# A two-layer hybrid decoder trunk on eight cores: a new opening of mixer 2, other load gates, and an order searched by shaking priorities

## The chip, the cores and the metric

The kernel runs on the eight cores of one Trainium2 chip, two dies of four cores. Every core does the same work on one batch element of eight; no core talks to another. The metric is the device time of the slowest core, in microseconds, as the median of several runs. One execution is also profiled, and all durations below are of that one.

## The reference

```python
for i in range(DEPTH):                      # DEPTH = 2
    h = rmsnorm(x, norm_mix_g[i])
    if i % 2 == 0:
        x = x + mlstm_mixer(h, ...)         # matrix memory, chunks with a carried state
    else:
        x = x + gla_mixer(h, ...)           # gated linear attention, chunks with a carried state
    h = rmsnorm(x, norm_ffn_g[i])
    x = x + square(relu(h @ w1[i])) @ w2[i] # D = 1024, D_FF = 4096
return rmsnorm(x, final_norm_g)             # x: (8, 2048, 1024) float32
```

Each mixer projects to q, k (512 wide each), v and an output gate (1024 wide each), runs four heads over the sequence with a state that is carried from chunk to chunk, normalises each head, multiplies by the gate and projects back.

## The kernel before

**Stages.** A core holds its `xT` (1024 x 2048, transposed) in SBUF all the time. Four stages follow one another: mixer 1, FFN of layer 0, mixer 2, FFN of layer 1. The 2048 tokens are cut into 4 groups of 512 and 16 chunks of 128. A mixer (`Mixer.run`) walks the 16 chunks; the state products, the gating and the head norm of a chunk (`S1`, `S2`, `P2a` to `P2c`, `S34`, `Cst`) are a chain across TensorE, VectorE and ScalarE, and projections of later tokens (`v`, `o`, `qk`, `op_`) are put between as filling (`fills`, L1255). Two DMA transposes on SP's queue belong to each chunk: `KX` makes the keys token-major (tiles `ktok_134`, `ktok_135`), `S7` brings the head outputs back (tile `hn` into `xn_44` to `xn_47`, dependency name `hnT`). The gates of the second mixer come from `z_F` (L1072): two matmuls, exponentials on ScalarE and eight scans on VectorE.

**FFN.** An FFN works through steps of 7 matrix products each (a seven-product scheme for 2x2 blocks). The weights come in slabs, one DMA on POOL's queue each, cast from float32 on the way (1 MB read, 512 KB landed), into slots `wraw_76` (slot 0) to `wraw_89` (slot 13); slot 1 is `wraw_77`, slot 4 `wraw_80`, slot 5 `wraw_81`. For each slab VectorE makes three sums (`sums`, tiles `wsum`). The first two steps run inside the last chunk of the mixer (`first_tiles`, L1458). `slot_of` (L1429) names the slot of the n-th slab; `loads` starts a slab as soon as the step that used its slot is over.

**Order.** No engine's order is written out by hand. Every `t.op` and `t.dma` appends a unit with its reads, writes and a cost in ns; `order` (L93) then makes a list schedule: `schedule` (L154) walks simulated time, looks at the next units of each engine in program order (48 on TensorE, ScalarE and VectorE, 24 on POOL, 4 on SP), and takes the ready one with the smallest priority. Priorities start as program order; after each pass `needed` (L139) replaces them by the latest start that the schedule allows. Of 8 passes the one with the earliest simulated end is emitted. Units that start in the first 60 us or the last 36 us keep program order. Each engine then runs its list strictly in that order, with semaphore waits made from the reads and writes alone. Simulated slab loads land at 0.29 KB per ns of a shared rate plus 4 us.

**Around the change.** Before the chunk loop of mixer 2, L1541 issues `z_F(1, 0)`, the q and k of two heads of group 1, then `v(0)`, `o(0)`, `v(1)`; `z_F(1, 1)` and the q and k of head 2 are filling of chunk 0. The out projection's eight loads (`wout_load`, L549, two staging buffers `wst_182` and `wst_183`, each followed by one multiply on VectorE) wait only for a free staging buffer. In `ffn_start` (L1439) slab 0 waits for gate 12 and slab 1 for gate 14; slabs 2 and 3 for the last head output of the mixer, and slabs 4 and 5 for nothing but their slot. Gate i (`Mixer.gate`, L1101) means: the head output of chunk i-1 and the keys of chunk i+1 have landed. The final norm of token groups 0 and 1 (`out_held`, L1563, with `stats_slots`) is hooked to steps 31 to 42 of the last FFN; each pair of rows ends in a store `outT<-xT` on SP's queue.

Of the kernel before, what the change touches and what calls it, by code (L numbers as in the profile page):

```python
# [28 lines left out]
class Trk:  # L29
# [4 lines left out]
    SLACK = 300.0  # L34
    PASSES = 8
    EDGES = 60000.0, 36000.0
    LEAD = dict(pe=-163, act=93, dve=82, pool=0, sp=0)
    HOP = dict(pe=145, act=100, dve=100, pool=120, sp=60)
    WIN = dict(pe=48, act=48, dve=48, pool=24, sp=4)

    def __init__(s, nc, es):
        s.nc, s.es = nc, es
        s.E = {}
        for name, eng in (("pe", nc.tensor), ("act", nc.scalar), ("dve", nc.vector),
                          ("pool", nc.gpsimd), ("sp", nc.sync)):
            s.E[name] = dict(eng=eng, sem=es.enter_context(nc.semaphore("s_" + name)), count=0, waited={})
        s.lastw, s.readers, s.iv, s.ovc = {}, {}, {}, {}
        s.nd = 0
        s.xsem = {}
        s.units, s.open = [], None  # L50

    def reg(s, key, lo, size, n=1, step=0):
        s.iv.setdefault(key, []).extend((lo + i * step, lo + i * step + size) for i in range(n))
# [11 lines left out]
    def op(s, ename, fn, r=(), w=(), ns=200, sig=True):  # L65
        reads = [k for k in r if k[0] != "B"]
        writes = [k for k in r if k[0] == "B"] + list(w)
        if s.open is None:
            s.open = dict(eng=ename, ins=[], r=[], w=[], ns=0, dma=None)
        u = s.open  # L70
        assert u["eng"] == ename
        u["ins"].append((fn, reads, writes, sig))
        u["r"] += reads
        u["w"] += writes
        u["ns"] += ns
        if sig:
            s.units.append(u)
            s.open = None

    def dma(s, qname, pairs, nbytes, r=(), w=(), sem=None):  # L80

        assert s.open is None
        u = dict(eng=qname, ins=[], r=list(r), w=list(w), ns=(950 if qname == "pool" else 450) * len(pairs),
                 dma=(pairs, nbytes), tok=None, xp=None, sem=sem)
        s.units.append(u)
        return u

# [5 lines left out]
    def order(s):  # L93

        lastw, readers = {}, {}
        for n, u in enumerate(s.units):
            preds = set()
            for k in u["r"]:  # L100
                if k in lastw:
                    preds.add(lastw[k])
            for k0 in u["w"]:
                for k in s.ov(k0):
                    if k in lastw:
                        preds.add(lastw[k])
                    preds.update(readers.get(k, ()))
            preds.discard(n)
            u["preds"] = preds
            for k in u["r"]:  # L110
                readers.setdefault(k, []).append(n)
            for k in u["w"]:
                lastw[k] = n
                readers[k] = []
        prio, best = list(range(len(s.units))), None
        for n in range(s.PASSES):
            seq, start, done = s.schedule(prio)
            end = max(done)
            if best is None or end < best[0]:
                best = end, seq  # L120
            prio = s.needed(seq, start, done)
            if not n:
                edges = [(m, -1e9) for m in seq if start[m] < s.EDGES[0]]
                edges += [(m, 1e9) for m in seq if start[m] > end - s.EDGES[1]]
            for m, far in edges:
                prio[m] = m + far
        s.model = best[0]
        return best[1]

    def hop(s, p, e):  # L130

# [145 lines left out]
def build():  # L277
# [22 lines left out]
    t = Trk(nc, es)  # L300
# [47 lines left out]
    wqk, _ = at("wqk", [128, KC, 1024], BF16, W[0])  # L348
# [38 lines left out]
    sd, _ = at("sd", [128, GS], F32)  # L387
# [29 lines left out]
    def slot(layer, g):  # L417
        return (g + 2 * layer) % 4
# [127 lines left out]
            t.dma("pool", [(dst[:, k0:k0 + step, :], v[:, k0:k0 + step, c0:c0 + 1024])],  # L546
                  step * 524288, w=[(nm, hf, k) for hf in range(2) for k in range(k0, k0 + step)])

    def wout_load(layer, k, q):  # L549
        v = (m_wout_d if layer == 0 else g_wout_d).rearrange("(k p) n -> p k n", p=128)  # L550
        i = k % len(wst[layer])
        halves = lambda ap: ap.rearrange("p (a n) -> p a n", n=GS)
        t.dma(q, [(wst[layer][i], halves(v[:, k, :]))], 524288, w=[("wst", layer, i)])
        t.op("dve", lambda e: e.tensor_scalar(
            out=halves(wout[:, k, :]), in0=wst[layer][i], scalar1=ong[:, layer * 8 + k:layer * 8 + k + 1],
            scalar2=None, op0=ALU.mult), r=[("wst", layer, i), ("ong",)], w=[("wout", k)], ns=750)
# [72 lines left out]
    def stats_slots(g, eng="pool"):  # L629
        return [lambda: sq_half(g, 0, eng), lambda: sq_half(g, 1, eng), lambda: sq_sum(g)]  # L630
# [296 lines left out]
    class Mixer:  # L927
# [313 lines left out]
        def qk(s, g, h):  # L1241
            return [lambda: s.qk_F(g, h, 0), lambda: s.qk_F(g, h, 1)]
# [12 lines left out]
        def fills(s, i, extra):  # L1255

            g, c = i // 4, i % 4
            v = s.v(i + 2) if i + 2 < NCH and not (s.m and i < 2) else []
            o = s.o(i + 1) if i + 1 < NCH else []
            ops = s.opq[:{0: 2, 1: 2, 2: 4, 3: 0}[c] if g == NG - 1 else 2]  # L1260
            del s.opq[:len(ops)]
            qk = lambda h: s.qk(g + 1, h)
            if g == 0:
                x = extra.get(i, [])
                if c == 0:
                    return x[:2] + o + x[2:] + v + (qk(2)[1:] if s.m else s.z(1, 1) + qk(2) if s.pre else [])
                if c == 1:
                    if s.m:
                        return o + qk(3)[1:]
                    return x[:2] + o + (qk(3) if s.pre else qk(0) + qk(1) + s.z(1, 1)) + x[2:] + v  # L1270
                if c == 2:
                    return o + v + ([] if s.m or s.pre else qk(2) + qk(3))
                return o + v
            if g < NG - 1 and c == 3:
                return qk(0) + qk(1) + s.z(g + 1, 1) + o + ops + v + qk(2) + qk(3)
            return o + v + ops + extra.get(i, []) if g == 1 and c == 0 else o + ops + v + extra.get(i, [])
# [152 lines left out]
    def slot_of(layer, n):  # L1429


        if layer == 0 and n >= 56:
            return (5, 0, 8, 3, 6, 7, 5, 8)[n - 56]
        i = (0, 4, 1, 5)[n] if n < 4 else (0, 4, 2, 3, 1, 5)[(n - 4) % 6]
        return i if layer == 0 or i == 5 else {0: 9, 4: 10, 1: 11, 2: 12, 3: 13}[i]

    ffn = [Ffn(L, lambda n, L=L: slot_of(L, n), ffn_steps(L)) for L in range(2)]
# [1 line left out]
    def ffn_start(layer):  # L1439

        hooks = {}

        def add(i, ns, fns):
            hooks.setdefault(i, []).extend(zip(ns, fns))
        mx, last, f = mix[layer], [("hnT", slot(layer, 3), 3)], ffn[layer]
        add(12, (-1,), [lambda: f.load(mx.gate(12))])
        add(14, (-1,), [lambda: f.load(mx.gate(14))])
        add(15, (0, 0), [lambda: f.load(last)] * 2)
        st = stats_slots(0)
        add(9, (5, 6), st[:2])  # L1450
        add(11, (0,), st[2:])
        add(11, (1, 2, 3, 4), f.xn_slots(0))
        add(12, (1, 3, 5), stats_slots(1))
        add(13, (1, 2, 3, 4), f.xn_slots(1))
        add(14, (1, 2, 3, 4), f.x_prep(0))
        return hooks

    def first_tiles(layer):  # L1458

        def f():  # L1460
            F = ffn[layer]
            set_ring([0, 1, 2, 3, 6])
            F.hold = True
            F.run(0, 2, {})
            F.hold = False
            for n in range(2):
                F.load()
        return [f]

    def mixer_to_ffn(mx, layer):  # L1470
# [68 lines left out]
    m1.KX(0)  # L1539
    m1.KX(1)  # L1540
    m1.z_F(1, 0)  # L1541
    for fn in m1.qk(1, 0) + m1.qk(1, 1) + m1.v(0) + m1.o(0) + m1.v(1):
        fn()
    set_ring(RING["g"])
    hooks = ffn_start(1)
    for k in range(KC):
        i, n = ((1, 11 + k), (2, k - 2), (3, k - 5))[(k > 1) + (k > 4)]
        hooks.setdefault(i, []).append((n, lambda k=k: wout_load(1, k, "pool")))
    m1.run({NCH - 1: first_tiles(1)}, hooks)
    mixer_to_ffn(m1, 1)  # L1550

# [11 lines left out]
    def out_held(g):  # L1563
        def f(k0):
            for k in range(k0, k0 + 2):
                stt(xT[:, k, tgs(g)], xT[:, k, tgs(g)], gains[:, 32 + k:33 + k], PB[ring["held"][g]][:], ALU.mult,
                    ALU.mult, [("gains",), ("B", ring["held"][g])], [("xT", k, g)], GS)
            store("sp", g, k0, 2, 0, GS)
        return [lambda k=k: f(k) for k in range(0, KC, 2)] + [lambda: free_bank(g)]
# [9 lines left out]

    F1 = ffn[1]  # L1580
    hooks = next_pair(1, 20)
    st, o = stats_slots(0, "dve"), out_held(0)
    hooks[31], hooks[32], hooks[33], hooks[34] = st[:2], st[2:] + o[:1], o[1:2], o[2:3]
    st, o1 = stats_slots(1, "dve"), out_held(1)
    hooks[35], hooks[36], hooks[38], hooks[40], hooks[42] = o[3:] + st[:2], st[2:] + o1[:1], o1[1:2], o1[2:3], o1[3:]
    F1.run(2, len(F1.steps) - 4, hooks)
    fin = F1.steps[-4:]
    F1.loads(len(F1.slabs))
# [100 lines left out]
```

How the kernel before makes its waits and increments, by code:

```python
    def _waits(s, ename, reads, writes):  # L211
        e = s.E[ename]
        pesem = s.E["pe"]["sem"]
        need = {}
        def add(sem, val):
            if ename == "pe" and sem is pesem:
                return
            if need.get(sem, 0) < val:
                need[sem] = val
        for k in reads:
            t = s.lastw.get(k)
            if t:
                add(*t)
        for k0 in writes:
            for k in s.ov(k0):
                t = s.lastw.get(k)
                if t:
                    add(*t)
                for sem, val in s.readers.get(k, {}).items():
                    add(sem, val)
        for sem, val in need.items():
            if e["waited"].get(sem, 0) < val:
                e["eng"].wait_ge(sem, val)
                e["waited"][sem] = val
# [10 lines left out]
    def emit(s):  # L246
# [11 lines left out]
                for o, i in u["dma"][0]:  # L258
                    c += 16
                    (e["eng"].dma_start_transpose if u["xp"] else e["eng"].dma_start)(out=o, in_=i).then_inc(sem, 16)
                if name:
# [15 lines left out]
def build():  # L277
# [1358 lines left out]
               j == 0, j == KC - 1, True, n)  # L1636
            gain(by[j], j, c0, n)
            if due and j > 1:
                due.pop(0)()
        rstd_fin(bank, c0, n)
        due += out_part(g, c0, n, bank, queues)
    for fn in due:
        fn()
    t.emit()
    for u in toks:
        nc.sync.wait_ge(*u["tok"])
    es.close()
    mybir.codegen_inst_isa_subclasses(nc)
    return nc
```

## Time and profile before

| | us |
|---|---|
| median of 3 runs | 1355.27 (1352.28 to 1355.8) |
| profiled execution, device time | 1354.16 |
| its span, slowest core (core 7) | 1353.1 |
| fastest core of it (core 1) | 1342.2 |
| TensorE busy, core 7 | 1314.0 (97%) |
| VectorE / ScalarE / POOL busy | 956.3 / 776.8 / 231.1 |

A span runs from a core's first to its last instruction; the device time has about 1 us around it. In the windows, "busy" is the union of an engine's instructions, PEclk the granted share of TensorE's full clock, DMA share the mean busy share of 16 DMA engines (it can exceed 1 where packets overlap). In the waits, the first name is the waiting instruction, the second the one that ended the wait.

### The profile page before, as it was taken

The numbers are of one execution on the slowest core, as the hardware profiler recorded it, in microseconds if no ns is written. First come the engines' busy times: TensorE is split into PE (matmuls) and PEld (weight loads), VectorE is DVE, ScalarE is ACT, GpSimd is POOL, SyncE is SP. The second block draws the span as 40 slices with busy tenths as digits, with TensorE's granted clock in tenths as the row PEclk, the third lists the DMA queues.
The fourth block names the chain that finished last, engine by engine and source line by source line (L and its number), as shares of the span: only waits on it lengthen the run. The fifth ranks groups of instructions, "written<-read, shape, count | busy, mean of one in ns | idle before, by whom it ended". The sixth has DMA issues, their size and how long they took to land.

```text
span 1353.1 us, 23147 instructions; the slowest of 8 cores (1342.2 to 1353.1 us)
## 1 busy us (share of the span) xinstructions
PE 1314.0 (97%) x6777; PEld 624.4 (46%) x6777; DVE 956.3 (71%) x2087; ACT 776.8 (57%) x1660; POOL 231.1 (17%) x260
## 2 busy tenths in 40 slices
PE   6999999999999999999999999999999999999997
PEld 2455454543444444444444454444444444444445
DVE  2399394966568988667756785879665788886847
ACT  2487666537249348167336877776552862943566
POOL 6020222011111112111010203221111111111113
PEclk9999999999999999999999999999999999999999
DMA  9944211468587687575756310122957847877963
GB/s 161 214 133 104 54 27 24 59 66 98 66 96 94 78 102 99 69 94 71 117 85 167 65 29 16 33 35 44 121 65 93 101 61 89 109 121 96 158 78 125
DMA packets 202347, 118.97 MB, mean 88 GB/s; under 512 B 53952, under 2 KB 187808, under 8 KB 202224
## 3 DMA queue, kind: packets, MB, share of 16 engines
q0 software_dynamic: 143728, 92.82, 50.3%
q1 hardware_dynamic: 57968, 24.41, 8.2%
q8 instruction: 57, 0.93, 0.3%
q14 instruction: 66, 0.54, 0.2%
q10 hardware_dynamic: 528, 0.26, 0.1%
HBM read 176.52 MB, written 8.39 MB: 137 GB/s over the span
## 4 chain that ended last, share of the span: by engine, by line
PE 88%; DMA 5%; DVE 2%; issue 2%; ACT 1%; POOL 1%; SPq 0%; DVEq 0%; ACTq 0%; POOLq 0%
PE ps L303 88%; DMA wraw_80<-w 2%; DMA wqk<-m_win 2%; DMA wraw_88<-w 1%; DMA ktok_134<-kx_187 0%; ACT og_144 L309 0%; DVE Cbf L1215 0%; POOL xT L1621 0%; POOL wqk L260 0%; DVE xT L313 0%; DVE hn L313 0%; DMA xn_47<-hn 0%; SPq L260 0%; ACT junk L309 0%; DVE tiny L317 0%
## 5 line engine op out<-in xcount | busy, mean ns | idle before, releaser
L309 ACT ACTIVATE ps<-ps 128x512 f32<-128x512 f32 x192 | 111.3, 584 | 199.3 <-PE ps L303 151.7
L313 DVE TENSOR_TENSOR xT<-ps,xT 128x512 f32<-128x512 f32 (+2 forms) x224 | 142.6, 649 | 106.0 <-PE ps L303 104.7
L309 ACT ACTIVATE rt<-ps 128x512 f32<-128x512 f32 x152 | 89.6, 592 | 55.3 <-PE ps L303 54.0
L309 ACT ACTIVATE sq<-xT 128x512 f32<-128x512 f32 x128 | 78.5, 627 | 29.9 <-DVE sd L313 14.9
L317 DVE SCALAR_TENSOR_TENSOR R_142<-R_142,egs,ps 128x256 f32<-128x256 f32 x112 | 53.1, 474 | 7.1 <-PE ps L303 5.8
L313 POOL TENSOR_TENSOR sd<-sd,sq 128x512 f32<-128x512 f32 x40 | 51.1, 1278 | 33.9 <-ACT sq L309 28.6
L309 ACT ACTIVATE junk<-ps 128x256 bf16<-128x256 f32 x128 | 48.9, 382 | 13.4 <-PE ps L303 5.8
L313 POOL TENSOR_TENSOR sd<-sq 128x512 f32<-128x512 f32 x8 | 10.6, 1324 | 245.6 <-ACT sq L309 193.7
L322 DVE CUSTOM_DVE_ANT_0 rt<-ps,rt 128x512 f32<-128x512 f32 x46 | 31.7, 689 | 18.9 <-PE ps L303 17.4
L303 PE MATMUL ps<-xn_44,wqk 128*128 128x512 bf16 x128 | 33.0, 412 | 11.1 <-DMA wqk<-m_win 10.9
L309 ACT ACTIVATE og_144<-og_144 128x512 f32<-128x512 f32 x60 | 37.4, 628 | 3.4 <-ACT og_144 L309 0.4
L309 ACT ACTIVATE og_145<-og_145 128x512 f32<-128x512 f32 x60 | 37.8, 631 | 2.6
L1215 DVE TENSOR_SCALAR Cbf<-R_142,egs 128x256 bf16<-128x256 f32 x90 | 33.3, 394 | 1.4
L1085 DVE TENSOR_TENSOR_SCAN NB<-ones_bf,NB 128x128 f32<-128x128 bf16 x64 | 26.7, 443 | 10.4 <-ACT NB L309 9.0
L309 ACT ACTIVATE tmp_157<-ps 128x512 f32<-128x512 f32 x37 | 21.9, 592 | 19.5 <-PE ps L303 18.9
L303 PE MATMUL ps<-wo,xn_46 128*128 128x512 bf16 x128 | 31.4, 393 | 1.4 <-ACT tiny L309 1.1
L309 ACT ACTIVATE sq_149<-xT 128x512 bf16<-128x512 f32 (+2 forms) x48 | 21.7, 495 | 18.1 <-DMA xT<-xT 9.7
L260 POOL DMA_DIRECT2D wraw_81<-w x22 | 19.3, 877 | 71.3 <-PE ps L303 23.3
L303 PE MATMUL ps<-xn_47,wout 128*128 128x512 bf16 x128 | 29.1, 379 | 1.7 <-DMA xn_47<-hn 1.6
L303 PE MATMUL ps<-wv,xn_47 128*128 128x512 bf16 x128 | 29.7, 379 | 0.6 <-DVE xT L313 0.6
L303 PE MATMUL ps<-xn_45,wqk 128*128 128x512 bf16 x128 | 30.1, 379 | 0.0
L303 PE MATMUL ps<-wo,xn_47 128*128 128x512 bf16 x128 | 30.1, 379 | 0.0
(1119 smaller groups left out, 3586.9 us busy)
## 6 DMA issues: line engine op xcount, KB each, us to landing
wraw_81<-w POOLq DMA_DIRECT2D x22, 512.0 KB, 8.5
outT<-xT SPq DMA_DIRECT2D x12, 512.0 KB, 5.3
wraw_76<-w POOLq DMA_DIRECT2D x11, 512.0 KB, 6.8
wraw_85<-w POOLq DMA_DIRECT2D x11, 512.0 KB, 6.5
wraw_86<-w POOLq DMA_DIRECT2D x11, 512.0 KB, 8.5
wraw_87<-w POOLq DMA_DIRECT2D x11, 512.0 KB, 7.0
wraw_80<-w POOLq DMA_DIRECT2D x10, 512.0 KB, 8.2
wraw_79<-w POOLq DMA_DIRECT2D x10, 512.0 KB, 8.2
```

Of the source, the lines that this page charges most:

```text
L260: (e["eng"].dma_start_transpose if u["xp"] else e["eng"].dma_start)(out=o, in_=i).then_inc(sem, 16)
L303: t.op("pe", lambda e: e.matmul(out, lhsT=lhsT, rhs=rhs, start=start, stop=stop, **kw), r=r, w=w, sig=sig, ns=max(cols, 64) * (1.7 if f32 ...
L309: t.op("act", lambda e: e.activation(out=out, in_=in_, func=func, **kw), r=r, w=w, ns=190 + 0.84 * n + (80 if acc is not None else 0))
L313: t.op(eng, lambda e: e.tensor_tensor(out=out, in0=in0, in1=in1, op=op), r=r, w=w, ns=170 + 1.03 * n if eng == "dve" else 200 + 2.2 * n)
L317: t.op("dve", lambda e: e.scalar_tensor_tensor(out=out, in0=in0, scalar=scalar, in1=in1, op0=op0, op1=op1), r=r, w=w, ns=200 + 1.07 * n)
L322: t.op("dve", lambda e: e._custom_dve(dve_ops.TENSOR_ADD_SAT, out=out, in0=in0, in1=in1, s0=3.0e38, s1=0.0), r=r, w=w, ns=170 + 1.03 * n)
L1085: t.op("dve", lambda e, cv=cv: e.tensor_tensor_scan(out=cv, data0=ones_bf[:], data1=cv, initial=0.0, op0=ALU.mult, op1=ALU.add), r=[("ones ...
L1215: t.op("dve", lambda e, h=h: e.tensor_scalar(out=Cbf[:, h, :], in0=R32[:, h, :], scalar1=ec[:, h:h + 1], scalar2=None, op0=ALU.mult), r=[( ...
```

## The change

The diff does six things. (1) The opening of mixer 2 also holds `z_F(1, 1)` and head 2 of group 1, and chunk 0 loses that filling. (2) The out projection's loads of mixer 2 are hooked two to a chunk, to the start of chunks 0 to 3, and those of chunks 1 to 3 wait for the chunk's gate. (3) Slabs 0 to 3 of each FFN wait for gates 12, 13, 14 and 15; slabs 4 and 5 wait for the last head output of the mixer; slots 1 and 5 swap their places in `slot_of`. (4) The final norm of groups 0 and 1 is hooked to slightly different steps, and its units carry `past`, a predecessor in the schedule (the last TensorE unit ahead of them in program order), and a fixed priority, their start in the first pass. `past` makes no semaphore wait. (5) A schedule is judged by `cost`, the mean end of three replays of its order with slab rates of 0.29, 0.25 and 0.27 KB per ns, landing times of 4, 2.5 and 1 us, and in the third up to 4 us more at random. (6) After the 8 passes, 500 times, the priorities of a part of the units in a stretch of 10 to 40 us are moved at random; what costs no more is kept. Stretches begin after 60 us and end 36 us before the end.

```diff
+    SHAKES = 500
+    REPLAYS = (0.29e3, 4000, 0), (0.25e3, 2500, 0), (0.27e3, 1000, 1)
...
         for n, u in enumerate(s.units):
-            preds = set()
+            preds = set() if u["past"] is None else {u["past"]}
...
-            end = max(done)
-            if best is None or end < best[0]:
-                best = end, seq
+            end, cost = max(done), s.cost(seq)
+            if best is None or cost < best[0]:
+                best = cost, prio, seq, start, end
             prio = s.needed(seq, start, done)
...
+                timely = {m: start[m] for m in seq if s.units[m]["past"] is not None}
+            for m, st in timely.items():
+                prio[m] = st
...
-        s.model = best[0]
-        return best[1]
+        rng, fixed = random.Random(1), {m for m, _ in edges}
+        for _ in range(s.SHAKES):
+            cost, prio, seq, start, end = best
+            span, dev, part = rng.choice((1e4, 2e4, 4e4)), rng.choice((300, 1000, 3000)), rng.choice((0.1, 0.3, 1))
+            at_ = rng.uniform(s.EDGES[0], end - s.EDGES[1])
+            prio = list(prio)
+            for m in range(N):
+                if at_ - span < start[m] < at_ and m not in fixed and rng.random() < part:
+                    prio[m] += rng.gauss(0, dev)
+            seq, start, done = s.schedule(prio)
+            cost = s.cost(seq)
+            if cost <= best[0]:
+                best = cost, prio, seq, start, max(done)
+        s.model = best[4]
+        return best[2]
...
+    def replay(s, seq, rate, land, seed):
...
+                hbm = max(hbm, st + 1500) + u["dma"][1] / (rate if slab else 0.29e3)
+                done[n] = hbm + (1200 if st < 60000 else land + seed * rng.uniform(0, 4000) if slab else 2500)
...
-    def wout_load(layer, k, q):
+    def wout_load(layer, k, q, gate=()):
...
-        t.dma(q, [(wst[layer][i], halves(v[:, k, :]))], 524288, w=[("wst", layer, i)])
+        t.dma(q, [(wst[layer][i], halves(v[:, k, :]))], 524288, r=gate, w=[("wst", layer, i)])
...
-                    return x[:2] + o + x[2:] + v + (qk(2)[1:] if s.m else s.z(1, 1) + qk(2) if s.pre else [])
+                    return x[:2] + o + x[2:] + v + (qk(2)[1:] if s.m else [])
...
-        i = (0, 4, 1, 5)[n] if n < 4 else (0, 4, 2, 3, 1, 5)[(n - 4) % 6]
+        i = (0, 4, 5, 1)[n] if n < 4 else (0, 4, 2, 3, 5, 1)[(n - 4) % 6]
...
-        mx, last, f = mix[layer], [("hnT", slot(layer, 3), 3)], ffn[layer]
-        add(12, (-1,), [lambda: f.load(mx.gate(12))])
-        add(14, (-1,), [lambda: f.load(mx.gate(14))])
-        add(15, (0, 0), [lambda: f.load(last)] * 2)
+        mx, f = mix[layer], ffn[layer]
+        for i in range(12, 16):
+            add(i, (-1,), [lambda i=i: f.load(mx.gate(i))])
...
             for n in range(2):
-                F.load()
+                F.load([("hnT", slot(layer, 3), 3)])
...
-    for fn in m1.qk(1, 0) + m1.qk(1, 1) + m1.v(0) + m1.o(0) + m1.v(1):
+    for fn in m1.qk(1, 0) + m1.qk(1, 1) + m1.z(1, 1) + m1.v(0) + m1.v(1) + m1.o(0) + m1.qk(1, 2):
...
-        i, n = ((1, 11 + k), (2, k - 2), (3, k - 5))[(k > 1) + (k > 4)]
-        hooks.setdefault(i, []).append((n, lambda k=k: wout_load(1, k, "pool")))
+        i = k // 2
+        hooks.setdefault(i, []).append((-1, lambda i=i, k=k: wout_load(1, k, "pool", m1.gate(i) if i else ())))
...
-    st, o = stats_slots(0, "dve"), out_held(0)
-    hooks[31], hooks[32], hooks[33], hooks[34] = st[:2], st[2:] + o[:1], o[1:2], o[2:3]
-    st, o1 = stats_slots(1, "dve"), out_held(1)
-    hooks[35], hooks[36], hooks[38], hooks[40], hooks[42] = o[3:] + st[:2], st[2:] + o1[:1], o1[1:2], o1[2:3], o1[3:]
+    for g, at_ in enumerate(((31, 31, 32, 32, 33, 34, 35, 35), (34, 34, 35, 36, 38, 40, 42, 42))):
+        for n, fn in zip(at_, out_timely(g)):
+            hooks.setdefault(n, []).append(fn)
```

## Rows read from the trace of the kernel before

**Rows 1.** The page's head and its busy times by engine, core 7
```profile
span 1353.1 us, 23147 instructions; the slowest of 8 cores (1342.2 to 1353.1 us)
...
PE 1314.0 (97%) x6777; PEld 624.4 (46%) x6777; DVE 956.3 (71%) x2087; ACT 776.8 (57%) x1660; POOL 231.1 (17%) x260
```

**Rows 2.** Spans and granted clock of four of the cores
```profile
core 1: 1342.2 us, clock 0.997
...
core 3: 1351.4 us, clock 0.996
...
core 5: 1350.5 us, clock 0.996
...
core 7: 1353.1 us, clock 0.995
```

**Rows 3.** Stretches of core 7: length, busy of each engine, PEclk, DMA share, GB/s
```profile
60.00:1300.00 1240.00, 1220.83 (x6143) 574.08 (x6142) 911.95 (x1994) 720.05 (x1530) 196.18 (x205) 1.00 0.58 83
280.00:320.00 40.00, 33.60 (x147) 14.50 (x146) 21.95 (x50) 15.13 (x27) 6.13 (x7) 0.96 0.90 98
400.00:500.00 100.00, 100.00 (x465) 45.28 (x464) 86.22 (x180) 58.99 (x109) 14.86 (x17) 1.00 0.73 88
700.00:752.00 52.00, 48.92 (x243) 23.13 (x242) 36.07 (x76) 34.46 (x84) 9.31 (x13) 0.97 0.66 152
840.00:860.00 20.00, 18.26 (x101) 9.23 (x100) 18.53 (x37) 15.03 (x42) 8.92 (x7) 1.00 0.20 41
1250.00:1270.00 20.00, 17.98 (x84) 7.86 (x83) 15.77 (x37) 13.46 (x26) 2.62 (x3) 1.00 1.17 201
```

**Rows 4.** The same view: core 1 first, then core 3
```profile
60.00:1300.00 1240.00, 1228.41 (x6192) 578.63 (x6191) 914.17 (x1996) 732.35 (x1548) 197.96 (x207) 1.00 0.59 84
...
1250.00:1270.00 20.00, 17.25 (x74) 7.20 (x71) 13.13 (x32) 11.40 (x21) 2.62 (x3) 0.91 1.18 200
```

**Rows 5.** The chain that ended last, core 7, 280 to 312 us: start, us, what
```profile
280.38 3.06 DMA xn_47<-hn
...
288.92 21.93 DMA wraw_80<-w
...
310.94 0.06 DVE wsum_0_102 L327
...
311.29 0.69 DVE rt L322
```

**Rows 6.** TensorE's waits, core 7, 280 to 320 us: total, times, longest
```profile
PE ps L303 <- DVE rt L322: 3.3, 1, 3.3
PE ps L303 <- DMA xn_47<-hn: 1.6, 1, 1.6
PE ps L303 <- DMA wraw_81<-w: 1.5, 1, 1.5
```

**Rows 7.** DMA issues of core 7, 1244 to 1256 us: count, size, median us to landing
```profile
outT<-xT SPq DMA_DIRECT2D x3, 512.0 KB, 10.1
...
wraw_88<-w POOLq DMA_DIRECT2D x1, 512.0 KB, 16.5
```

**Rows 8.** The same view, core 7, 1178 to 1194 us
```profile
wraw_88<-w POOLq DMA_DIRECT2D x1, 512.0 KB, 5.7
```

**Rows 9.** TensorE's waits, 700 to 752 us: core 7, then core 5
```profile
PE ps L303 <- ACT tiny L309: 1.1, 1, 1.1
PE ps L303 <- DVE og_145 L313: 0.8, 1, 0.8
PE ps L303 <- DMA ktok_134<-kx_187: 0.5, 1, 0.5
...
PE ps L303 <- DMA ktok_134<-kx_187: 2.8, 1, 2.8
```

**Rows 10.** POOL's wait for a gate in mixer 1, among all waits of core 7
```profile
POOL wraw_80 L260 <- DMA xn_47<-hn: 21.0, 1, 21.0
```

**Rows 11.** DMA issues of core 7, 264 to 282 us
```profile
xn_47<-hn SPq DMA_TRANSPOSE x2, 4.0
```

More of the change, by code:

```diff
@@ L1 @@
+import random
 import numpy as np
@@ L49, in __init__ @@
         s.xsem = {}
-        s.units, s.open = [], None
+        s.units, s.open, s.timely, s.last_pe = [], None, False, None
     def reg(s, key, lo, size, n=1, step=0):
@@ L68, in op @@
         if s.open is None:
-            s.open = dict(eng=ename, ins=[], r=[], w=[], ns=0, dma=None)
+            s.open = dict(eng=ename, ins=[], r=[], w=[], ns=0, dma=None,
+                          past=s.last_pe if s.timely else None)
         u = s.open
@@ L76, in op @@
         if sig:
+            if ename == "pe":
+                s.last_pe = len(s.units)
             s.units.append(u)
@@ L83, in dma @@
         u = dict(eng=qname, ins=[], r=list(r), w=list(w), ns=(950 if qname == "pool" else 450) * len(pairs),
-                 dma=(pairs, nbytes), tok=None, xp=None, sem=sem)
+                 dma=(pairs, nbytes), tok=None, xp=None, sem=sem, past=None)
         s.units.append(u)
@@ L114, in order @@
                 readers[k] = []
-        prio, best = list(range(len(s.units))), None
+        prio, best, N = list(range(len(s.units))), None, len(s.units)
         for n in range(s.PASSES):
             seq, start, done = s.schedule(prio)
-            end = max(done)
-            if best is None or end < best[0]:
-                best = end, seq
+            end, cost = max(done), s.cost(seq)
+            if best is None or cost < best[0]:
+                best = cost, prio, seq, start, end
             prio = s.needed(seq, start, done)
@@ L124, in order, with cost @@
                 edges += [(m, 1e9) for m in seq if start[m] > end - s.EDGES[1]]
+                timely = {m: start[m] for m in seq if s.units[m]["past"] is not None}
+            for m, st in timely.items():
+                prio[m] = st
             for m, far in edges:
                 prio[m] = m + far
-        s.model = best[0]
-        return best[1]
+        rng, fixed = random.Random(1), {m for m, _ in edges}
[13 more added lines that the diff above has]
+        return best[2]
+    def cost(s, seq):
+        return sum(s.replay(seq, *c) for c in s.REPLAYS) / len(s.REPLAYS)
+    def replay(s, seq, rate, land, seed):
+        done, free, hbm, xq = [0.0] * len(seq), {e: 1500.0 for e in s.E}, 0.0, 0.0
+        rng = random.Random(seed)
+        for n in seq:
+            u = s.units[n]
+            e = u["eng"]
+            st = max([free[e]] + [done[p] + s.hop(p, e) for p in u["preds"]])
+            free[e] = st + (u["ns"] if u["dma"] else max(u["ns"] - max(s.LEAD[e], 0), 60))
+            if u["dma"] and u["xp"]:
+                free[e] = st + 1300
+                pk, b = 64 if u["xp"] == "hn" else 32, max(st + 1000, xq)
+                slow = min(pk, int(max(0.0, hbm - b) / 200))
+                xq = b + slow * 200 + (pk - slow) * 18
+                done[n] = xq + 950
+            elif u["dma"]:
+                slab = bool(u["sem"])
+                hbm = max(hbm, st + 1500) + u["dma"][1] / (rate if slab else 0.29e3)
+                done[n] = hbm + (1200 if st < 60000 else land + seed * rng.uniform(0, 4000) if slab else 2500)
+            else:
+                done[n] = st + u["ns"] - min(s.LEAD[e], 0)
+        return max(done)
     def hop(s, p, e):
@@ L1581, in build, with out_timely, timely @@
     hooks = next_pair(1, 20)
-    st, o = stats_slots(0, "dve"), out_held(0)
-    hooks[31], hooks[32], hooks[33], hooks[34] = st[:2], st[2:] + o[:1], o[1:2], o[2:3]
-    st, o1 = stats_slots(1, "dve"), out_held(1)
-    hooks[35], hooks[36], hooks[38], hooks[40], hooks[42] = o[3:] + st[:2], st[2:] + o1[:1], o1[1:2], o1[2:3], o1[3:]
+    def out_timely(g):
+        def timely(fn):
+            t.timely = True
+            fn()
+            t.timely = False
+        return [lambda fn=fn: timely(fn) for fn in stats_slots(g, "dve") + out_held(g)]
+    for g, at_ in enumerate(((31, 31, 32, 32, 33, 34, 35, 35), (34, 34, 35, 36, 38, 40, 42, 42))):
+        for n, fn in zip(at_, out_timely(g)):
+            hooks.setdefault(n, []).append(fn)
     F1.run(2, len(F1.steps) - 4, hooks)
```

## The prediction

> **What bounds the kernel now.** I read the page's head first: TensorE is busy 1314.0 of 1353.1 us [rows 1], so only what keeps it waiting or slows it can be won. Next the spans of the cores: the same program takes 1342.2 us on core 1 and 1350.5 to 1353.1 on cores 3, 5 and 7 [rows 2]. The metric is the slowest core, so about 11 us are a matter of which core gets its data late. The stretches then say where. Between 60 and 1300 us core 7's TensorE idles 1240 - 1220.8 = 19.2 us [rows 3], core 1's 1240 - 1228.4 = 11.6 us [rows 4]. In the middle of an FFN (400 to 500 us) there is no idle at all at full clock [rows 3]. The idle sits in a few places: 280 to 320 us (40 - 33.6 = 6.4), 700 to 752 (3.1), 840 to 860 (1.7) and 1250 to 1270 (2.0), all in [rows 3]. Two of them also show a lower granted clock, 0.96 and 0.97: for a while after the idle TensorE runs at its 1.2 GHz level, which costs (1 - 0.96) x 40 = 1.6 us and (1 - 0.97) x 52 = 1.6 us of full-rate work.
>
> Last the chain of waits, for the cause. At the start of the first FFN it runs through the load of `wraw_80`, issued at 288.92 and 21.93 us under way; then through a sum of that slab on VectorE, then `rt` on VectorE, and only then TensorE goes on [rows 5]. TensorE's 3.3 us wait is for `rt` [rows 6], an evacuation that doesn't read the slab: it stands behind the slab's sum in VectorE's fixed order. A late slab thus stops TensorE before TensorE needs it. At 1250 us a slab took 16.5 us while group 1's stores, at a median of 10.1, were under way [rows 7]; the same slot took 5.7 us at 1178 to 1194 us [rows 8]. The DMA share there is 1.17 [rows 3].
>
> **The change, part by part.** No instruction is added or removed on an engine: loads, stores, matmuls and evacuations keep their numbers, and the search costs no device time. So each part is the stall it takes away, or makes.
>
> A. *Slabs 2 and 3 earlier.* Before, six slabs are issued in a burst from 284 us, because slabs 2 and 3 wait for the last head output, which lands at 280.38 + 3.06 = 283.4 us [rows 5]. After, slabs 2 and 3 follow the head outputs of chunks 13 and 14, a chunk or two earlier; the burst shrinks from six to four. The load that held up the chain was fourth of the six and becomes second. With 21.93 us for a fourth place, one place is some 5 us, so it lands about 10 us earlier, against a wait of 3.3. The wait for `wraw_81`, 1.5 us [rows 6], goes with it, since that slab is now third and among the early ones. Gain on core 7: 3.3 + 1.5 + 1.6 (clock) = 6.4 us. Bounds: 6.4 and 0, since VectorE's order is made anew and the sum may again stand ahead of an evacuation. I take 6.4, because the margin is three times the wait. Slabs 4 and 5 now wait for the last head output, but slabs that follow it were issued only after it already.
>
> B. *Stores spread.* Before, group 1's stores fall together with slab loads near 1250 us. Nothing in the next instructions needs stored data, so `needed` gives these units late priorities and they bunch; with `past` and a priority of their first-pass start they go out one per step or two (steps 36, 38, 40, 42). Gain on core 7: its 2.0 us of idle [rows 3]. Core 3 has 20 - 17.25 = 2.75 us of idle and a clock of 0.91 there, another 1.8 us [rows 4]: 4.5 us. Bounds: 2.0 gained, or as much lost if a spread store meets a slab in a phase that had none. I take 2.0 on core 7. The VectorE work of these units is the same; it lies under TensorE work, where VectorE is busy 86 of 100 us in a full stretch [rows 3], so its cover is thin: if it fails, each pair of multiplies delays one evacuation by their own length, under 2 us.
>
> C. *Mixer 2's opening.* The idle of 700 to 752 us is a string of short waits: ScalarE's `tiny` 1.1, VectorE's `og` 0.8, the key transpose 0.5, on core 5 the last is 2.8 [rows 9]. VectorE and ScalarE are busy 36.1 and 34.5 of 52 us [rows 3]: neither is full, chains are in each other's way. `z_F(1, 1)`, with its scans and exponentials, moves ahead of the chunk chain, to where TensorE has dense projections; and the out projection's loads no longer land in the same moments as the transposes, since six of eight wait for the chunk's gate. Idle 3.1 and clock 1.6 give 4.7 us at most. The other bound is a loss: chunk 0 has two q/k tiles less to fill TensorE with, so a chain that was covered may show, again up to the 3.1 us. I take a gain of 3, two thirds, since transposes and gates are separate causes and both are treated. The added waits stand on POOL's queue. Behind them are only later loads of the same kind, and in the last chunks of a mixer the next slab and the sums of squares for the next norm. POOL already sat 21.0 us at such a gate [rows 10] and no wait of TensorE named POOL, so I cost this at nothing; without that cover it is one chunk's delay of a norm.
>
> D. *The shakes.* What remains of core 7's idle after A, B and C is 19.2 - 4.8 - 2.0 - 3.1 = 9.3 us, chains between engines such as those of 840 to 860 us [rows 3]. The search may remove these as far as its costs resemble the chip. Nothing in this trace shows how far: bounds are 9.3 gained, and 5 lost, half as much again as now. I take 3 gained, a third: the waits are single ones of about 1 us, and a replay must get an order right to a few hundred ns to see them.
>
> *Sum.* Core 7's span: 1353.1 - 6.4 - 2.0 - 3.0 = 1341.7. That is near core 1's 1342.2 - 3.0 = 1339.2, which never had A or B, so the cores come together and no other core is left far behind. Less 3 for D: 1338.7. The slowest of eight cores will still meet some late slab; I put back three tenths of A and B, 2.5 us: 1341.2. The profiled execution has 1354.16 - 1353.1 = 1.1 us around the span: 1342.3. Its time lies 1.1 us under the median of the runs and inside their scatter of 1352.28 to 1355.8, so I add nothing: **1342 us**, 13 us or 1.0% under the median.
>
> A page of the Trainium skill speaks against parts A and B: HBM Reference, Specifications (TRN2), says that two cores of a domain share its bandwidth and that each still gets about 358 GB/s when both stream. At 1250 us the records show 201 GB/s landed or stored [rows 3], below that share even if the float32 reads behind cast slabs are counted, which makes it some 300, an estimate. By that rule the loads were not short of bandwidth, and spreading them would give A and B nothing. The rows show 16.5 us against 5.7 for the same load, so the measurement speaks for a shortage of something, whether or not of HBM.
>
> **The rivals.**
> 1. *The lateness only moves.* The bytes are the same and the DMA share is high throughout (0.73 in a quiet FFN stretch [rows 3]); a store between two slabs delays a third, and VectorE stops for it somewhere else. Then C's 3 us is all: 1354.2 - 3 = 1351. For it: any new VectorE order has sums ahead of evacuations. Against it: core 1 ran the same bytes without either stall. Chance 0.17.
> 2. *The shakes give most of D.* 8 of 9.3 rather than 3, and nothing left of A and B: 1342.3 - 5 - 2.5 = 1335. For it: the waits are the same on fast and slow cores, as a model can know them. Chance 0.15.
> 3. *The shakes keep nothing that the chip sees*, and only the written edits act: 1342.3 + 3 = 1345. Chance 0.13; inside the forecast's own range.
> 4. *Slower.* One mechanism: an order fitted to replays puts slab sums ahead of TensorE's evacuations by small margins all through the FFNs, and on the slowest core real landings overrun them. One such stall costs 3.3 + 1.6 = 4.9 us as at 312 us. The kernel has over a hundred slabs. Gains of 12 are outweighed from three stalls on one core; with four the time is 1342.3 + 4 x 4.9 = 1362, or 1358 where C's gain and D's hold better. The earlier slabs add a smaller cost of the same sign: a head transpose takes 4.0 us rather than 3.06 with a slab under way [rows 5, 11], and TensorE waits for the last one already. Against it: two of the three replays land slabs later or slower than the old assumption. Chance 0.08.
>
> **How the numbers follow.** The forecast (1338 to 1347) has the remaining 0.47; with rival 3 it is 0.60. About 0.3%, 4 us, is what a measurement of this kernel can tell from no change, so faster means under 1351.2. Forecast, rivals 2 and 3 are all faster, 0.75; rival 1 at 1351 lies on the edge, a third of it faster: 0.81. Same: the rest of rival 1 and a little of rival 4: 0.12. Slower: 0.07. The range takes most of rival 2 and most of rival 1: 1333 to 1352.
>
> **What would show it.** A: no TensorE wait for `rt` or a slab between 290 and 320 us, and slabs 2 and 3 landed before 283 us. B: stores of group 1 spread over some 40 us, and no slab over 12 us near them. C: less than 2 us of idle and a clock of 1.00 in the 50 us after mixer 2 starts. D: idle of core 1 between 60 and 1300 us under 8 us. The cores' spans would lie within 5 us of each other. It is wrong if the spread of the cores stays near 11 us, or if TensorE's waits for VectorE in the FFNs exceed today's.

## The result and the profile after

The changed kernel takes 1341.07, 1343.00 and 1343.51 us where the kernel before takes a median of 1354.89: a ratio of 0.9912 with a 95% interval of 0.9891 to 0.9933, 11.9 us less. The forecast was 1342. Executions in which a die ran at a lowered clock are left out, here two of the changed kernel's five, and where only one or two remain, the dies that kept their clock are compared as well, each by its longest core. All ratios are turned into us with 1354.

The cores of the profiled execution, to be read beside [rows 2]:

```profile
core 0: 1334.5 us, clock 0.998
...
core 1: 1338.3 us, clock 0.997
...
core 3: 1339.0 us, clock 0.998
...
core 5: 1340.0 us, clock 0.998
...
core 7: 1335.8 us, clock 0.999
```

The cores have come together, 1334.5 to 1340.0 where it was 1342.2 to 1353.1, and the fast ones are faster too. Stretches of core 5, now the slowest, answer to [rows 3] (length, busy of each engine, PEclk, DMA share, GB/s):

```profile
60.00:1300.00 1240.00, 1229.94 (x6207) 579.97 (x6206) 913.56 (x1999) 730.50 (x1551) 198.19 (x207) 1.00 0.61 84
270.00:320.00 50.00, 49.50 (x230) 22.33 (x229) 34.69 (x80) 28.96 (x57) 6.12 (x7) 1.00 0.72 80
690.00:740.00 50.00, 50.00 (x253) 23.97 (x251) 31.62 (x67) 34.67 (x76) 7.45 (x10) 1.00 0.55 110
1235.00:1260.00 25.00, 23.89 (x111) 10.52 (x110) 18.00 (x44) 18.21 (x34) 3.50 (x4) 1.00 1.11 149
```

From the slowest core of before to the slowest of after, TensorE's idle between 60 and 1300 us falls from 19.2 to 10.1 us, 9.1 less, and the mean clock rises from 0.995 to 0.998, which is some 4 us of full-rate work over 1340 us (the third decimal is worth 1.3 us). Together that is the 13.1 us between the spans. The first FFN's start idles 0.5 us instead of 6.4, mixer 2's start not at all instead of 3.1, both at full clock.

All of the idle that went was in those places. The three treated stretches (the first FFN's start, mixer 2's start and the stores, taken as 270 to 330, 680 to 755 and 1225 to 1300 us) hold 11.5 us of it on core 7 before and 1.9 on core 5 after; everything else between 60 and 1300 us holds 7.7 before and 8.1 after.

POOL's loads around the first FFN's start, core 5 (start, us, instruction, idle before):

```profile
260.44 1.06 POOL L310 DMA_DIRECT2D wraw_81<-w  x1 [10.76 <-issue]
271.84 0.88 POOL L310 DMA_DIRECT2D wraw_77<-w  x1 [10.34 <-DVE xT L363]
282.56 0.87 POOL L310 DMA_DIRECT2D wraw_76<-w  x1 [9.85 <-DVE wsum_1_94 L377]
```

Slabs 2 and 3 (`wraw_81`, `wraw_77`) start a chunk apart, well before the last head output; only then the shortened burst begins. The old mechanism has not died out. The chain that ended last on core 5, first near 400 us, then near 1240 us:

```profile
388.66 13.83 DMA wraw_77<-w
...
402.58 0.06 DVE wsum_0_93 L377
...
402.92 0.69 DVE rt L372
...
1231.93 10.16 DMA wraw_85<-w
...
1243.74 0.05 DVE wsum_2_119 L377
...
1244.07 1.29 DVE rt L372 x2
```

A late slab, its sum, an evacuation behind the sum, then TensorE, as in [rows 5]; but each now costs TensorE 1.0 to 1.1 us, not 3.3.

### The profile page after: what moved, and what is told of

It reads as the page before. It is cut to its first block, busy times and chain, and to the rows that moved or that the text cites. A ratio compares the mean times of both kernels' runs of the same rounds, so it can differ in the third digit from the quotient of the medians.

```text
span 1340.0 us, 23091 instructions; the slowest of 8 cores (1334.5 to 1340.0 us)
## 1 busy us (share of the span) xinstructions
PE 1307.9 (98%) x6777; PEld 623.6 (47%) x6777; DVE 955.2 (71%) x2087; ACT 775.6 (58%) x1660; POOL 231.3 (17%) x260
## 4 chain that ended last, share of the span: by engine, by line
PE 87%; DMA 5%; DVE 3%; issue 3%; ACT 1%; POOL 1%; SPq 0%; DVEq 0%; ACTq 0%; POOLq 0%
PE ps L353 87%; DMA wv<-m_win 2%; DMA wraw_77<-w 1%; DMA wraw_85<-w 1%; DMA xT<-m_wout 0%; DVE xT L363 0%; ACT junk L359 0%; DVE R_142 L367 0%; DMA xn_47<-hn 0%; POOL wqk L310 0%; POOL wv L310 0%; POOL xT L1678 0%; DVE xn_45 L367 0%; DVE hn L363 0%; DVE hn L367 0%
## 5 line engine op out<-in xcount | busy, mean ns | idle before, releaser
L363 POOL TENSOR_TENSOR sd<-sq 128x512 f32<-128x512 f32 x8 | 10.1, 1266 | 240.4 <-ACT sq L359 195.9
L353 PE MATMUL ps<-xn_44,wqk 128*128 128x512 bf16 x128 | 31.5, 394 | 12.1 <-DMA wqk<-m_win 11.5
L1135 DVE TENSOR_TENSOR_SCAN NB<-ones_bf,NB 128x128 f32<-128x128 bf16 x64 | 29.8, 474 | 10.1 <-ACT NB L359 6.7
L359 ACT ACTIVATE sq_149<-xT 128x512 bf16<-128x512 f32 (+2 forms) x48 | 21.6, 497 | 19.0 <-DMA xT<-xT 10.6
L359 ACT ACTIVATE tmp_157<-ps 128x512 f32<-128x512 f32 x37 | 22.0, 594 | 17.1 <-PE ps L353 16.7
L359 ACT ACTIVATE tmp_158<-ps 128x512 f32<-128x512 f32 x35 | 20.7, 593 | 17.9 <-PE ps L353 17.3
L353 PE MATMUL ps<-wo,xn_47 128*128 128x512 bf16 x128 | 30.1, 379 | 0.2 <-DVE og_144 L363 0.2
```

Of the source, the lines that this page charges most:

```text
L353: t.op("pe", lambda e: e.matmul(out, lhsT=lhsT, rhs=rhs, start=start, stop=stop, **kw), r=r, w=w, sig=sig, ns=max(cols, 64) * (1.7 if f32 ...
L359: t.op("act", lambda e: e.activation(out=out, in_=in_, func=func, **kw), r=r, w=w, ns=190 + 0.84 * n + (80 if acc is not None else 0))
L363: t.op(eng, lambda e: e.tensor_tensor(out=out, in0=in0, in1=in1, op=op), r=r, w=w, ns=170 + 1.03 * n if eng == "dve" else 200 + 2.2 * n)
L1135: t.op("dve", lambda e, cv=cv: e.tensor_tensor_scan(out=cv, data0=ones_bf[:], data1=cv, initial=0.0, op0=ALU.mult, op1=ALU.add), r=[("ones ...
```

## The experiments

**The edits without the search, and the search without the edits.** The first keeps every edit of the program, with `SHAKES = 0` and the passes judged by the simulated end; the second puts the new `order`, `cost` and `replay` on the old program.

```diff
-    SHAKES = 500
+    SHAKES = 0
...
-            end, cost = max(done), s.cost(seq)
+            end = cost = max(done)
```

> The changed kernel with its edits to the program (opening, gates, slot order, spread stores) but without the 500 shakes, and with its 8 passes judged by the simulated end as before. Theory of the prediction: the edits carry the gain, 6.4 + 2 + 3 us on the slowest core, so this lies some 10 us under the kernel before, near 1345 us, and is 2 to 4 us slower than the changed kernel. No wait of TensorE for a slab at the start of the first FFN and none bunched with stores near 1250 us. Rival, the search carries the gain: 1350 to 1355 us, with new waits of TensorE for VectorE in places that the kernel before did not have.

> The program of the kernel before, with nothing changed but the search: three replays judge the passes, then 500 shakes. Theory of the prediction: 3 us or less under the kernel before on every core, with the six-slab burst at 284 us and the bunched stores still there, so near 1352 us and the cores still some 10 us apart. Rival, the search carries the gain: 1342 to 1346 us, because an order that is judged with late slabs has the sums of slabs behind the evacuations, so that the same late slabs stop nothing.

Measured: the edits alone 0.9954 (0.9939 to 0.9969), 6.2 us; the search alone 0.9979 (0.9967 to 0.9992), 2.8 us. The sum is 9.0, both together gave 11.9, so either may be worth more beside the other; the interval of each is some 2 us to either side, and the 2.9 us between them are not shown. The search alone came out as its first theory had it (2.8 us, cores 11 us apart), the edits carry most of the gain but not 10 us, and neither rival came.

The search alone mends the first FFN's start: the burst of six slabs is still there (on core 5 issued from 281.8 us on, up to 18.4 us to landing), but the cores idle only 0.2 to 1.4 us from 270 to 330 us. It does not mend mixer 2's start, where they idle 3.8 to 5.4 us from 680 to 755 us. In the old opening its order still waits for the key transpose, `ktok`, on core 2 (TensorE's waits, 680 to 755 us):

```profile
PE ps L353 <- DMA ktok<-kx: 2.1, 1, 2.1
PE ps L353 <- ACT tiny L359: 1.1, 1, 1.1
PE ps L353 <- DVE og L363: 0.8, 1, 0.8
```

**Each part alone**, without the search: the kernel before with part A (slab gates and slots), with part B (stores spread), with part C (opening of mixer 2, gated loads). The edits are those of the diff above, one part at a time.

> The kernel before with part A alone (slabs 0 to 3 at gates 12 to 15, slabs 4 and 5 at the last head output, slots 1 and 5 swapped), 8 passes, no search. Theory: the waits for the slab and for VectorE between 300 and 320 us go, 6.4 us on the slowest core of before; cores 3 and 5 still have the stall at 1250 us, so the median falls by 2 to 6 us. Rival: 0, the lateness turns up at the next slabs.

> The kernel before with part B alone (final norm of groups 0 and 1 at the new steps, with the schedule predecessor and the fixed priority), 8 passes, no search. Theory: the stores spread, the waits between 1240 and 1280 us go, 2 to 4.5 us on the four late cores; the median falls by 1 to 3 us, held up by the first FFN's start. Rival: 0 or a loss, as a store now meets slabs in another step and VectorE stops there.

> The kernel before with part C alone (the new opening of mixer 2 and the gated loads of the out projection), 8 passes, no search. Theory: of the 4.7 us of waits and low clock in the 50 us after mixer 2 starts at least 3 go, on every core alike, so the median falls by 3 to 5 us. Rival: the string of short waits is remade by the new order and moves into the next chunks: under 1.5 us.

Measured: A alone has one execution that counts, 1354.12 us, beside a median of 1353.6 for the kernel before, and by dies 1352.3 us (5 dies) beside 1352.4 (37): nothing, as its rival had it. B alone 0.9974 (0.9964 to 0.9983), 3.5 us, a little over its theory. C alone 0.9979 (0.9970 to 0.9989), 2.8 us, a little under its own. Together that is 6.3 us, what the edits give at once. B did its local work: between 1235 and 1280 us only one core still waits, for 0.6 us. So did part A. Stretches of the slowest core, core 4, of the kernel with A alone:

```profile
60.00:1300.00 1240.00, 1221.11 (x6146) 573.40 (x6145) 911.03 (x1993) 721.05 (x1532) 196.57 (x205) 1.00 0.61 83
270.00:330.00 60.00, 60.00 (x291) 27.70 (x290) 45.31 (x101) 36.08 (x71) 7.89 (x9) 1.00 0.74 86
1225.00:1300.00 75.00, 72.17 (x334) 32.30 (x333) 55.03 (x115) 35.31 (x64) 10.53 (x12) 1.00 0.88 118
```

No idle is left at the first FFN's start, yet the core idles 18.9 us in all, where core 7 of before had 19.2. Against that core it idles 0.8 us more at the bunched stores (2.8 in all), and the rest of the 6.4 is back in short waits: 1.2 us more from 60 to 110 us, 2.3 from 330 to 680, 1.6 from 680 to 755, 0.5 from 900 to 1225. C alone also works where it is made and gives back later. Core 1, the first and second stretch of mixer 2, with C alone and then in the changed kernel:

```profile
680.00:755.00 75.00, 74.27 (x382) 36.20 (x380) 52.21 (x107) 51.84 (x123) 16.50 (x18) 1.00 0.52 118
755.00:900.00 145.00, 141.72 (x724) 68.93 (x723) 108.16 (x222) 101.56 (x247) 27.93 (x22) 0.99 0.19 29
```

```profile
680.00:755.00 75.00, 74.83 (x389) 36.65 (x387) 49.73 (x103) 50.91 (x120) 15.97 (x18) 1.00 0.57 123
755.00:900.00 145.00, 143.12 (x736) 69.93 (x735) 114.89 (x227) 105.30 (x255) 27.77 (x22) 1.00 0.18 32
```

Before, core 1 idled 3.2 us in the first of these stretches and 1.9 in the second. With C alone it is 0.7 and 3.3, at a clock of 0.99; with the search 0.2 and 1.9. The order is made anew for the whole program after every edit, so a stall taken away here can return as others there; beside the edits the search removes some of those. Core 1 shows it in two longer stretches, with the edits alone and then in the changed kernel:

```profile
60.00:1300.00 1240.00, 1227.92 (x6182) 577.31 (x6181) 913.04 (x1994) 726.55 (x1544) 199.35 (x207) 1.00 0.60 83
330.00:680.00 350.00, 346.90 (x1601) 155.79 (x1600) 251.54 (x539) 177.08 (x321) 52.70 (x64) 1.00 0.72 87
```

```profile
60.00:1300.00 1240.00, 1231.22 (x6212) 580.55 (x6210) 912.88 (x1999) 730.69 (x1553) 197.99 (x207) 1.00 0.61 84
330.00:680.00 350.00, 348.29 (x1611) 157.06 (x1610) 251.85 (x545) 178.82 (x325) 51.86 (x63) 1.00 0.74 87
```

Its idle from 330 to 680 us is 0.6 us before, 3.1 with the edits alone and 1.7 with the search. Over the cores whose records are complete, the idle outside the three treated stretches is 6.8 to 8.0 us before, 8.7 to 12.0 with the edits alone and 6.3 to 8.6 in the changed kernel.

**Does VectorE's order turn a late slab into a stop?** One number of the old planner is changed and nothing else: it expects slabs 6 us later.

```diff
-                done[n] = hbm + (1200 if st < 60000 else 4000 if u["sem"] else 2500)
+                done[n] = hbm + (1200 if st < 60000 else 10000 if u["sem"] else 2500)
```

> The kernel before with one number of its planner changed: simulated slabs land 10 us after their transfer rather than 4, in the 8 passes as before, no search and no other edit. The loads are issued by the same rules. Theory, VectorE stops at the sum of a late slab because the order expected it sooner: the sums move back, the waits for rt at 312 and 1260 us go though the bursts and bunched stores stay, and the late cores gain 4 to 8 us. Rival, the late slabs themselves are what TensorE waits for: the waits stay, now as waits for a slab or its sums, and the time is that of before within 2 us.

VectorE in the kernel before, core 7 (start, us, instruction, idle before it and what ended it): it stands idle for 3.86 us at the first sum of `wraw_80`, and the evacuation that TensorE waits for comes next. The third line is the first matmul that reads the slab: it starts 11.6 us after the slab landed.

```profile
310.94 0.43 DVE L327 TENSOR_TENSOR wsum_0_102<-wraw_80 128x512 bf16<-128x512 bf16 x1 [3.86 <-DMA wraw_80<-w]
311.29 0.68 DVE L322 CUSTOM_DVE_ANT_0 rt<-ps,rt 128x512 f32<-128x512 f32 x1
...
322.43 1.03 PE L303 MATMUL ps<-xs_0_52,wraw_80 128*128 128x512 bf16 x4
```

With the later expectation, on core 7: the loads issued from 282 to 300 us (their time to landing), then two stretches and TensorE's waits between 330 and 680 us.

```profile
DMA to landing us min/median/max: 8.9/16.5/20.8
```

```profile
270.00:330.00 60.00, 59.99 (x279) 26.94 (x277) 43.59 (x101) 38.53 (x74) 8.81 (x11) 1.00 0.77 90
680.00:755.00 75.00, 67.27 (x328) 31.50 (x327) 45.48 (x98) 40.16 (x94) 9.61 (x14) 0.98 0.64 127
...
PE ps L303 <- ACT ps L309: 5.2, 8, 1.0
```

The burst is there, a slab takes 20.8 us, and TensorE does not stop: 59.99 of 60 us busy. Near 1260 us too, where four stores still go out within 12 us (10 before), it has no wait left. So the theory holds for the stops: the slab was soon enough for TensorE and too late only for the place of its sum. The expected gain did not come all the same: the ratio is 1.0069 (1.0050 to 1.0087), 9.3 us slower. Mixer 2's start idles 7.7 us instead of 3.1, and in the rest of the same FFN, from 330 to 680 us, core 7 idles 5.7 us where it had 0.6: TensorE now waits for ScalarE's evacuations. An assumption that takes the stops at late slabs away remade every other order as well, that of the FFN included.

**What the search is judged by, its luck, and its length.** The changed kernel with one replay at the old slab timing; with another seed; with 1000 shakes.

```diff
-    REPLAYS = (0.29e3, 4000, 0), (0.25e3, 2500, 0), (0.27e3, 1000, 1)
+    REPLAYS = (0.29e3, 4000, 0),
...
-        rng, fixed = random.Random(1), {m for m, _ in edges}
+        rng, fixed = random.Random(2), {m for m, _ in edges}
...
-    SHAKES = 500
+    SHAKES = 1000
```

> The changed kernel, with its 500 shakes, but judged by a single replay with the old slab timing (0.29 KB per ns, 4 us). Theory: if judging by other slab timings is what makes the order hold on the slow cores, this shows again waits of 1 to 3 us for VectorE behind late slabs on some cores, a spread of the cores over 6 us, and 3 to 6 us more than the changed kernel. Rival, the edits have made the slabs early enough for any order: the same as the changed kernel within 2 us.

> The changed kernel with another seed for the shakes. Theory: the gain does not hang on one lucky order, so within 2 us of the changed kernel, with the remaining waits of TensorE in other places. Rival, luck: 1346 us or more. It also says how much of a difference between two searched kernels is the seed alone.

> The changed kernel with 1000 shakes rather than 500; the first 500 are the same. Theory: what the replays can see is mostly found by 500, so 0 to 2 us less than the changed kernel. Rival, the search still gains at a steady rate: 3 us or more less, with less idle of TensorE in the mixers on every core. Second rival, it now fits the replays and not the chip: as the changed kernel or slower.

Measured: one replay 0.9948 (0.9930 to 0.9967), 7.0 us, cores 1336.9 to 1345.2; seed 2 0.9922 (0.9903 to 0.9940), 10.6 us; 1000 shakes 0.9933 (0.9917 to 0.9949), 9.1 us. The gain does not hang on one seed. Twice the shakes find nothing more that the chip sees: the idle between 60 and 1300 us is 8.7 us (median of the cores with all their records), 8.9 in the changed kernel. The first stretch that may be shaken, 60 to 110 us, is worse: core 2 idles 2.5 us there at a clock of 0.97, core 3 of the changed kernel 1.9 at 1.00.

```profile
60.00:110.00 50.00, 47.46 (x333) 25.49 (x332) 42.92 (x111) 38.06 (x102) 8.96 (x7) 0.97 0.59 156
```

A single replay gives less than any of the three searches with several, and its slowest core has the expected sort of wait, TensorE held for 2.5 us by an evacuation at 1166 us while a core 8 us faster has none there. The chain of that core (start, us, what) goes from a late slab through its sum and VectorE's `rt` to ScalarE's evacuation:

```profile
1143.93 18.17 DMA wraw<-w
...
1162.20 0.06 DVE wsum L377
...
1163.88 0.59 DVE rt L372
...
1165.47 0.59 ACT ps L359
```

The intervals of one replay and of the others overlap, though, and each is a single searched order, so that several replays are worth 2 to 5 us is likely and not shown beyond doubt.

**One part taken out**, with the search.

> The changed kernel with part A undone (slabs 2 and 3 wait again for the last head output, slots as before), with the search. First theory (the written edits add up): the stall of 300 to 320 us is back, 3 to 6 us slower than the changed kernel. Second theory, formed on the runs so far (TensorE stops at a late slab only where VectorE's order has its sum too early, and the search with late slabs moves the sum): the burst of six is back in the loads, but TensorE waits for VectorE or a slab between 290 and 320 us for under 1 us on every core, and the time is within 3 us of the changed kernel.

> The changed kernel with part B undone (final norm of groups 0 and 1 at the old steps, no schedule predecessor, no fixed priority), with the search. First theory: the stores bunch again near 1250 us and the late cores lose 2 to 4 us there, so 2 to 4 us slower than the changed kernel. Second theory: the search has put the sums later there too, within 2 us of the changed kernel. The run with the search alone still had that stall, 2.4 to 4 us on four cores, which speaks for the first.

> The changed kernel with part C undone (old opening of mixer 2, ungated loads of the out projection), with the search. First theory: the waits and the low clock of 700 to 752 us are back on every core, 4 us or more, and the time is 4 to 7 us over the changed kernel. Rival: the search finds an order for the old opening, and only the part that hangs on slow transposes, 0.5 to 3 us, remains. The run with the search alone lost 7 to 9 us in that stretch, which speaks for the first.

Measured: without A only two executions that count, 1348.12 and 1352.18 us, beside a median of 1353.4 before (by dies 1346.1 us, 6 dies, beside 1351.6); without B 0.9956 (0.9936 to 0.9976), 6.0 us; without C 0.9973 (0.9959 to 0.9987), 3.7 us. Beside the changed kernel's 11.9 us that is 6 to 8 us less in the cases with an interval. It cannot all be put down to the parts. These three kernels and the one with 1000 shakes were measured together, and their four traces are the only ones of fourteen in which TensorE's clock dips to 0.81 without idle (last section). Beside the 1000 shakes (median 1344.69, by dies 1342.7), which shares those dips, C is worth 5.8 us, B 3.3 and, by dies, A 3.5, each from one searched order, where another seed alone makes 1.3 us. C is needed for the reason given: the wait for the transpose is back (core 7, 680 to 755 us).

```profile
PE ps L353 <- DMA ktok<-kx: 2.2, 1, 2.2
PE ps L353 <- ACT tiny L359: 1.1, 1, 1.1
```

Without A the second theory was right about the place: core 2's burst takes up to 19.7 us to land and TensorE idles 1.1 us from 270 to 330 us, not 6.4; on core 4 the waits for a slab and for VectorE add up to 1.1 us, just over its bound. Its time, within 3 us, was not met. Part of the loss is a clock of 0.94 from 600 to 650 us, one of those dips. Without B the stores did not do it: cores idle 0 to 0.8 us from 1225 to 1300 us, on cores with all their records, and 7.1 us (median) from 60 to 1300, less than the changed kernel's 8.9. On the slowest core four of those dips stand in its place. What A and B are worth beside the search is therefore open.

## Why the prediction was right, and where its parts were not

The sum was right: 1342 forecast, 1343.0 the middle of three executions; 11.9 us forecast below the profiled 1354.16, 11.9 measured as a ratio. So were the places: no wait for `rt` or a slab at the first FFN's start, group 1's stores spread over 41 us (1232.7 to 1273.8), mixer 2's start at full clock without idle, the cores close together. Two signs were missed narrowly: the cores lie 5.5 us apart in the profiled execution and 7.8 and 7.4 in the other two, not within 5, and core 1 still idles 8.8 us between 60 and 1300 us, not under 8 (D's). The split was wrong in two terms that cancel, and that they cancel so exactly is luck.

*The edits, A + B + C less the 2.5 us put back, were to give 8.9; without the search they gave 6.2.* The step that failed is part A's term: "I take 6.4, because the margin is three times the wait." The margin was real (on core 5 `wraw_80` now lands 9.3 us after its issue rather than 21.93), and the wait went, but A alone moved the span by nothing, since the slowest core was then another one that still met the stores, and the order made anew added short waits. Such waits had no term of their own: the 2.5 us put back stood for late slabs. Rival 1 has the size of A alone, not the way: of what came back at most 1.8 us was VectorE holding up the FFN's evacuations, the rest mostly waits in the mixers and for ScalarE. B, put at 2.0, gave 3.5 alone. C was priced at two thirds of its 4.7 us; its stretch gave all of it on every core, and without the search a part came back in the next 150 us.

*D was to give 3; it gave 5.7 beside the edits, 2.8 without them.* With the other seed and the longer search it is 4.4 and 2.9, so "a third of what is left" was near the low end. But it did not come from what was left: outside the treated stretches the slowest core idles 7.7 us before and 8.1 after, so of the 9.3 us that D was to work on only the 1.6 us wait for a head output [rows 6], which lies in the first stretch, can be gone. What the search removes beside the edits is what the edits themselves had stirred up (8.7 to 12.0 us there), which the row of 9.3 us in the kernel before could not show. D's size was about right and its mechanism was not.

*B's sign that no slab would take over 12 us was wrong:* beside the spread stores one still takes 13.5 us. DMA issues of core 5, 1230 to 1240 us:

```profile
outT<-xT SPq DMA_DIRECT2D x1, 512.0 KB, 7.3
wraw_86<-w POOLq DMA_DIRECT2D x1, 512.0 KB, 13.5
```

The page HBM Reference of the Trainium skill (Specifications) gives each core about 358 GB/s when both cores of a domain stream, by which spread loads would gain nothing at 201 GB/s. A slab still takes 13.5 us where 149 GB/s are landed or stored (1235 to 1260 us), as one took 16.5 at 201 [rows 3, 7], so a rate below 358 GB/s doesn't say that a load lands soon; but the gain came from where the sums stand as much as from when the slabs land, so B neither proves nor refutes it. Rival 4, slower through sums placed too early, did not come with several replays; the kernel with one replay shows a small form of it. One reading was off without harm to the sum: the 4.0 us of [rows 11] is the median of a transpose of 4.9 us with a slab under way and of the one of 3.06 itself.

## What to carry to other kernels

A wait that one engine shows can belong to the order of a second one: look at what stands ahead of the late instruction on its engine, and ask whether the load was late for the work or for the place of a preparation. When a planner remakes the whole order after each edit, local stalls read from a trace are not terms of a sum (8.9 us here, where the times of the parts alone add up to 6.3 and the edits at once give 6.2); time the parts alone and left out before crediting one. Judge a searched order by several timings of what varies on the chip, and expect differences of 1 to 3 us here between searches of equal standing.

## What the runs showed of the hardware

TensorE's clock has dips that do not follow idle. In the kernel without B, cores 2 and 3 both ran at a granted 0.81 in the same 15 us; on core 2 TensorE had been busy without a gap at full clock just before (690 to 708 us, first line), and it stays busy all through the dip (second line, 709 to 724 us). The third line is core 2 of the kernel with 1000 shakes, in a dip with next to nothing moved by DMA.

```profile
690.00:708.00 18.00, 18.00 (x89) 8.20 (x88) 10.43 (x22) 8.07 (x15) 3.33 (x5) 1.00 0.74 108
709.00:724.00 15.00, 15.00 (x61) 6.45 (x60) 7.14 (x16) 9.71 (x23) 0.00 (x0) 0.81 0.54 125
...
537.00:549.00 12.00, 12.00 (x48) 4.93 (x47) 7.47 (x16) 2.33 (x4) 0.00 (x0) 0.81 0.01 1
```

One such stretch costs (1 - 0.81) x 15 = 2.9 us and shows no idle at all; core 2 of the kernel without B had four of them (near 540, 716, 746 and 1252 us), 11 us, and a mean clock of 0.989. They do not belong to one order: the kernels without A, B and C and the one with 1000 shakes, which were measured together, all have them, in different places, and the profiled executions of the other ten kernels, before and after among them, have none. The kernel before, measured beside those four, had a mean clock of 0.994 over all its cores, and 0.996 beside the other experiments. What sets the dips off is open.

The stretches of the kernel before at the 1.2 GHz level, by contrast, each came behind or amid waits: on core 7 a mean of 0.59 from 312 to 315.4 us, behind the one wait of 3.3 us [rows 6], and again near 735 us amid the string of [rows 9]. Such a string is not enough by itself, for core 0 waited 0.8, 1.1 and 1.6 us there and kept its clock. So idle alone does not rank two orders of this kernel: the mean clock of each core must stand beside it, and only kernels measured together should be compared by it.
